# Sums of squares of queries and keys by a row product with 32 columns of ones on four column groups, then turned

## What is computed

```python
proj = hn @ w_in                                   # 256 x 4112
qkv = silu(causal_depthwise_conv(proj[..., :3 * 1024], conv_w))
def l2norm(x):
    return x * rsqrt(sum(x * x, axis=-1) + 1e-6)   # over the 128 features of a head
q = l2norm(heads(qkv[..., :1024])) * 128 ** -0.5
k = l2norm(heads(qkv[..., 1024:2048]))
v = heads(qkv[..., 2048:])
o = chunk_gated_delta_rule(q, k, v, g, beta)
```

## Time and profile before

| what | value |
|---|---|
| median of 3 runs | 1313.11 us (1312.80 to 1314.77) |
| the profiled execution's own time | 1314.13 us |
| its span, first to last instruction | 1312.4 us |
| mean granted clock of PE, 1 is full speed | 0.993 |
| PE busy | 1266.1 us, 96% of the span |
| DVE, ACT, POOL busy | 832.5, 666.7, 59.0 us |
| loads from HBM | 209.14 MB, 160 GB/s over the span |
| sums of squares on PE (L956) | 64 records (each product of float32 is two), 82.6 to 105.1 us |

### The profile page before, as it was taken

The page is one execution under the profiler, slowest core; times in us unless marked ns, Lnnn a source line. Parts: engine busy times, 40 slices in busy tenths (PEclk is TensorE's granted clock), DMA queues, the critical chain, the costliest instruction groups (busy, mean ns, idle before and its releaser), DMA issues.

```text
span 1312.4 us, 23625 instructions
## 1 busy us (share of the span) xinstructions
PE 1266.1 (96%) x9832; PEld 1184.1 (90%) x9832; DVE 832.5 (63%) x1133; ACT 666.7 (51%) x933; POOL 59.0 (4%) x102
## 2 busy tenths in 40 slices
PE   5999999999999999999999999999999988999997
PEld 5998898999998998899999999889999977999996
DVE  4875447655556555655556589987665566767664
ACT  4873656544445554444444554545454355654452
POOL 4000001000000001000000000010000010000000
PEclk9999999999999999999999999999999999999999
DMA  7650106665555644555554754443545642555550
GB/s 245 202 161 33 68 3 207 209 192 180 183 185 168 198 156 143 170 190 184 183 187 151 225 174 149 148 141 102 184 149 182 196 152 80 186 185 180 187 192 33
DMA packets 160471, 211.41 MB, mean 161 GB/s; under 512 B 5541, under 2 KB 143219, under 8 KB 160387
## 3 DMA queue, kind: packets, MB, share of 16 engines
q1 hardware_dynamic: 157299, 202.77, 48.2%
q0 software_dynamic: 2048, 7.37, 1.5%
q10 hardware_dynamic: 1040, 0.07, 0.1%
HBM read 209.14 MB, written 1.05 MB: 160 GB/s over the span
## 4 chain that ended last, share of the span: by engine, by line
PE 84%; DVE 8%; ACT 3%; issue 2%; DMA 1%; POOL 1%; DVEq 0%; SPq 0%; POOLq 0%; ACTq 0%
PE bank L306 25%; PE bank L309 25%; PE bank L310 25%; DVE wlo L300 2%; PE bank L1180 2%; PE bank L1200 1%; PE bank L1736 1%; ACT whi L292 1%; ACT common L544 1%; PE bank L1208 1%; DVE xlo L615 1%; DMA raw<-in_dn_w_in 1%; DVE common L2272 1%; PE bank L1818 1%; PE bank L2292 1%
## 5 line engine op out<-in xcount | busy, mean ns | idle before, releaser
L300 DVE TENSOR_TENSOR wlo<-raw,whi 128x2048 fp32r<-128x2048 f32 x191 | 437.0, 2290 | 240.2 <-ACT whi L292 239.8
L306 PE MATMUL bank<-xhi,whi 128*128 128x256 f32 x1824 | 524.7, 288 | 11.7 <-DVE xlo L615 11.3
L309 PE MATMUL bank<-xlo,whi 128*128 128x256 f32 x1824 | 517.9, 284 | 0.0
L310 PE MATMUL bank<-xhi,wlo 128*128 128x256 f32 x1824 | 517.8, 284 | 0.0
L292 ACT ACTIVATE whi<-raw 128x2048 fp32r<-128x2048 f32 x191 | 364.6, 1910 | 175.0 <-PE bank L306 121.6
L306 PEld LDWEIGHTS bank<-xhi,whi 128*128 128x128 f32 x1824 | 351.8, 193 | 17.5 <-issue 13.2
L309 PEld LDWEIGHTS bank<-xlo,whi 128*128 128x128 f32 x1824 | 351.8, 193 | 2.8 <-issue 1.2
L310 PEld LDWEIGHTS bank<-xhi,wlo 128*128 128x128 f32 x1824 | 351.7, 193 | 0.0
L306 PE MATMUL bank<-whi,hhi 128*128 128x512 f32 x392 | 154.0, 393 | 3.3 <-DVE hlo L2729 2.5
L309 PE MATMUL bank<-wlo,hhi 128*128 128x512 f32 x392 | 153.5, 392 | 0.0
L310 PE MATMUL bank<-whi,hlo 128*128 128x512 f32 x392 | 153.2, 391 | 0.0
(11 more groups left out here) (334 smaller groups left out, 1522.7 us busy)
## 6 DMA issues: line engine op xcount, KB each, us to landing
raw<-in_mlp_w_up SPq DMA_DIRECT2D x32, 1024.0 KB, 5.4
raw<-in_mlp_w_down SPq DMA_DIRECT2D x32, 1024.0 KB, 4.8
raw<-in_w_in SPq DMA_DIRECT2D x22, 1024.0 KB, 5.2
raw<-in_w_up SPq DMA_DIRECT2D x22, 1024.0 KB, 5.1
raw<-in_dn_w_in SPq DMA_DIRECT2D x16, 1024.0 KB, 5.7
raw<-in_w_gate SPq DMA_DIRECT2D x16, 1024.0 KB, 5.4
raw<-in_mb_w_in SPq DMA_DIRECT2D x12, 1024.0 KB, 5.1
raw<-in_w_down SPq DMA_DIRECT2D x11, 1024.0 KB, 4.8
```

What stands on the lines that cost most here:

```text
L300: nc.vector.tensor_tensor(wlo[:, s, :], raw[:, V % RAW, :], f32(whi[:, s, :]), ALU.subtract).then_inc(lo_ready, 1)
L306: ins = pe.matmul(o, shi, mhi, start=first, stop=False, skip_group_check=True)
L309: pe.matmul(o, shi, mlo, start=False, stop=False, skip_group_check=True)
L310: return pe.matmul(o, slo, mhi, start=False, stop=last, skip_group_check=True)
```

## The change

Per x (keys, queries) 16 products of one column become 8 products with `ones[:, 0:32]` as the stationary operand and a whole tile of squares (256 tokens) as the moving one. Four column groups `c` of 32 columns write four strips of 32 partitions of one bank, two heads `j` per strip, 256 columns each. ACT copies the bank to SBUF (`act_square_sums`, 128x512), PE turns four 128x128 blocks of it back into the same bank (`pe_turn_sums`), so that tokens lie on partitions again, and DVE picks every 32nd column in two instructions of 128x8.

The places: key sums after unit 9, turned after unit 10, and the query sums right behind; they are turned after unit 11. The copies stand in ACT's steps 10 and 11, behind the copy of the weight unit and before silu. Both sums and turns of the keys use bank 7 (`O[3]`), those of the queries bank 5 (`O[1]`, which was free until `pe_setup`). Nothing of the sums is left in `pe_setup` and `dve_setup`.

```diff
-            uss = {x: O[3].use() for x in (1, 0)}
+            uss = {1: O[3].use(), 0: O[1].use()}
+            ust = {1: O[3].use(), 0: O[1].use()}
+            sum_rows = [common[:, 512 * x:512 * x + 512] for x in range(2)]
...
-            def pe_square_sum(pe, x, n):
-
-                if n == 0 and uss[x].n:
-                    pe.wait_ge(uss[x].freed, uss[x].n)
-                t, hd = n // HN, n % HN
-                return pe.matmul(uss[x].ps[:, n:n + 1], sq[:, 8 * x + hd, t * P:(t + 1) * P], ones[:, 0:1],
-                                 start=(n == 0), stop=(n == 15), skip_group_check=True)
+            def pe_square_sums(pe, x):
+
+                use = uss[x]
+                if use.n:
+                    pe.wait_ge(use.freed, use.n)
+                pe.wait_ge(squares[4 * x + 3].sem, squares[4 * x + 3].value)
+                for j in range(2):
+                    for c in range(4):
+                        ins = pe.matmul(use.ps[32 * c:32 * c + 32, T * j:T * j + T], ones[:, 0:32],
+                                        sq[:, 8 * x + 2 * c + j, :], start=(j == 0), stop=(j == 1),
+                                        skip_group_check=True)
+                ins.then_inc(use.filled, 1)
+
+            def act_square_sums(act, x):
+                act.wait_ge(uss[x].filled, uss[x].n + 1)
+                nc.scalar.activation(sum_rows[x], uss[x].ps[:, :], ACT.Copy).then_inc(uss[x].freed, 1)
+
+            def pe_turn_sums(pe, x):
+                pe.wait_ge(uss[x].freed, uss[x].n + 1)
+                if ust[x].n:
+                    pe.wait_ge(ust[x].freed, ust[x].n)
+                for n in range(4):
+                    ins = pe.transpose(ust[x].ps[:, n * P:n * P + P], sum_rows[x][:, n * P:n * P + P], ident[:, :])
+                ins.then_inc(ust[x].filled, 1)
...
+                    elif u == 9:
+                        pe_square_sums(pe, 1)
+                    elif u == 10:
+                        pe_turn_sums(pe, 1)
+                        pe_square_sums(pe, 0)
+                    elif u == 11:
+                        pe_turn_sums(pe, 0)
...
                     split_hi(act, units[u])
+                    if u >= 10:
+                        act_square_sums(act, 11 - u)
...
-                elif u == 10:
-                    dve_square_means(dve, 1)
+                elif u >= 10:
+                    dve_square_means(dve, 11 - u)
...
-                dve.wait_ge(uss[x].filled, uss[x].n + 1)
-                nc.vector.tensor_scalar(msn[:, 16 * x:16 * x + 16], uss[x].ps[:, 0:16], EPS, None, ALU.add)\
-                    .then_inc(uss[x].freed, 1)
+                dve.wait_ge(ust[x].filled, ust[x].n + 1)
+                turned = ust[x].ps[:, :].rearrange("p (j t c r) -> p j t c r", j=2, t=NT, c=4)
+                heads = msn[:, 16 * x:16 * x + 16].rearrange("p (t c j) -> p j t c", t=NT, c=4)
+                for j in range(2):
+                    ins = nc.vector.tensor_scalar(heads[:, j], turned[:, j, :, :, 0], EPS, None, ALU.add)
+                ins.then_inc(ust[x].freed, 1)
...
                 pe_gram(pe, 1)
-                proj.pe_turn(pe)
                 pe_cross(pe, 1)
...
                 dve_first(dve, 0)
-                proj.dve_cum(dve)
                 dve_first(dve, 1)
```

More of the change, by code:

```diff
@@ L961, in pe_in @@
                 for u in range(12):
[L962 to L970, removed]
+                    gemm_features(pe, units[u], uses[u], xhi, xlo)
                     if u == 0:
@@ L1101, in pool_in @@
                     cs = slice(16 * x, 16 * x + 16)
-                    pool.wait_ge(uss[x].freed, uss[x].n + 1)
+                    pool.wait_ge(ust[x].freed, ust[x].n + 1)
                     nc.gpsimd.tensor_tensor(rsq[:, cs], msn[:, cs], mhalf[:, 0:16], ALU.pow).then_inc(roots[x].sem, 1)
             return Part(pe=pe_in, act=act_in, dve=dve_in, pool=pool_in, uc=(una, ugc, roots, gates_spread),
-                        pe_turn=pe_query_sums, act_copy=lambda act: finish_unit(act, 11),
-                        dve_cum=lambda dve: dve_square_means(dve, 0))
+                        act_copy=lambda act: finish_unit(act, 11))
         def z_block(j, bank):
```

## The result

| | before | after |
|---|---|---|
| median, runs side by side | 1313.94 us (1312.80 to 1315.51, 4 runs) | 1304.35 us (1303.89 to 1305.48, 4 runs) |
| ratio, 95% interval | | 0.9934 (0.9920 to 0.9947) |
| profiled execution: time, span | 1314.13, 1312.4 us | 1304.77, 1303.0 us |
| mean granted clock of PE | 0.993 | 0.998 |

What follows compares the result with a forecast made beforehand. PE was taken to bound the kernel, on the path for 84% of the span. Removing 8.60 us and adding 3.16 us gave -5.44 us, so 1313.1 - 5.4 = 1307.7 us, range 1306.0 to 1311.2 us.

Steps and rivals of the forecast that it cites:

- Key sums, 3.37 us, and query sums, 3.49 us, removed: On PE, one-column sums go: 3.37 us out of unit 10 and 3.49 us out of `pe_setup`.
- The slow stretch behind them, 1.74 us: PE work after the query sums, 105.18 to 109.03 us, returns to full clock: 1.74 us less.
- A set of sums, 1.04 us: Added on PE, twice: 16 passes on four column groups plus tile change there and back, 1.04 us a set.
- Turning, 0.54 us: Added on PE, twice: four transposes at 0.44 us, with 0.1 us for going in and out.
- Nobody is late: ACT's copies have 2.3 and 3.0 us of slack, DVE and bank 5 0.3 us; PE waits for none.
- my tightest place: Second gram product waiting for bank 5, free at 3.75 us and reached at 4.05 us: slack 0.3 us.
- First decays at 97.1 us, third 4.4 us earlier, first key product 5.4 us earlier: Expected in the changed profile: first decays hardly earlier than 97.30 us, third decays and first key product earlier as named.
- the sum of 5.44 us: Net on PE: 3.16 us added less 8.60 us removed, -5.44 us.
- PE's program after `pe_setup` is unchanged and shifts as a whole: Everything on PE behind `pe_setup` keeps its program and only moves with the net of -5.44 us.
- another slow stretch of the clock vanishing too: Rival: one more slow stretch of the clock goes, about 1306.0 us; chance 0.05.
- two groups of 64 columns side by side: In the old profile, 64-column tiles run 1.86 times as fast; four groups taken for the square sums, 0.86 us of passes.
- The slower case: Rival at the two sets of 16 passes: groups run serially with exposed weight loads, 3.2 us more, 1316.3 us; chance 0.03.

Runs made afterwards that it cites:

- the spread sums: Kernel before, with its 16 one-column query sums spread between the products of unit 11: 1311.51 us, ratio 0.9987.
- keys only: Kernel before, with only the key sums in the new form and the query sums left in the setup: 1311.04 us, ratio 0.9980.
- on the whole array: Changed kernel, with a 128-wide stationary operand and no column groups side by side: 1311.04 us, ratio 0.9977 to the kernel before.

## Why the forecast was too small

**Point by point, what was asked of the profile.**

1. *Key sums, 3.37 us, and query sums, 3.49 us, removed.* The query sums are right. The key sums were worth a little more, 9.21 + 5.84 - 2 x 5.75 = 3.55 us: the first product of unit 11 too came 0.08 us late behind them (91.46 to 91.66 us, where a product takes 0.12), and I had taken unit 11 as undisturbed.
2. *The slow stretch behind them, 1.74 us.* Right for these two traces, and settled by the spread sums: 1.68 us in the trace, -1.82 +- 0.98 us in the times. In one of the three traces with the old query sums it is 3.3 us, so in the mean over executions the term may be too small.
3. *A set of sums, 1.04 us.* It is 1.19 us. The passes side by side were right to the hundredth (4 x 0.216 = 0.86 us for 16 passes); the change to the narrow tile and back is 0.33 us, not 2 x 0.09. The row I took it from showed the way into tiles of 64 columns only, and I doubled it.
4. *Turning, 0.54 us.* It is 97.22 - 96.79 = 0.43 us, 0.11 us less, since the change of tile is within the 1.19 us. With 3., 0.1 us more than forecast in all, and with 1. the sum is where it was.
5. *Nobody is late.* PE has no idle time at either turning, and the second gram product doesn't wait for bank 5, my tightest place. DVE is through with the query sums at 100.4 us and PE is at that product at about 100.7 us: the slack of 0.3 us is as forecast.
6. *First decays at 97.1 us, third 4.4 us earlier, first key product 5.4 us earlier.* 97.22 us; 102.51 us, 4.3 us earlier against the same records of before; 104.81 instead of 110.10 us, 5.3 us earlier.

The distance to the start of the span hides a part of it: in the trace of the kernel after, unit 9 already starts 0.2 us later (76.63 instead of 76.42 us), ahead of anything that was changed. From there to the first key product it is 5.49 us less, and 5.50 us in the other pair of traces. So for `pe_setup` the sum of 5.44 us held to a tenth. DVE shows the same; its first instruction on the key product (L1513 of before) starts at 105.94 instead of 111.23 us.

**The step that failed** is one sentence of the prediction: "PE's program after `pe_setup` is unchanged and shifts as a whole." The program is unchanged, but it didn't shift as a whole. The same instructions, after against before:

| place, time of before | shift so far | what stands there |
|---|---|---|
| end of `pe_setup`, 111 us | -5.3 us | the change itself, 5.5 us, less the 0.2 us from ahead of it |
| inside the rounds of 64x64, 146 us | -6.0 us | a shorter wait of PE |
| end of the rounds, 165 us | -6.1 us | |
| 170 us | -7.5 us | half clock of before missing |
| 202 us | -8.8 us | half clock of before missing |
| 300 us | -8.4 us | some of it given back |
| 1093 us | -9.7 us | half clock of before missing |

So behind the change these two traces come apart by another 4.4 us; in the mean of all runs it is 1.9 us (7.4 - 5.5).

*The wait in the rounds* belongs to the change. PE's weight loads in the rounds; the bracket is idle time with nothing that the profile shows to wait for. Before, in the run shown first:

```profile
144.42 1.51 PEld L1200 LDWEIGHTS bank<-common 64*64 64x64 f32 x48 [1.20 <-issue]
...
150.15 0.20 PEld L1208 LDWEIGHTS bank<-ident,dn_x 64*64 64x64 f32 x4 [2.01 <-issue]
```

after (L1217 and L1225 are L1200 and L1208 of before):

```profile
139.09 0.83 PEld L1217 LDWEIGHTS bank<-common 64*64 64x64 f32 x25 [0.52 <-issue]
...
144.88 0.48 PEld L1225 LDWEIGHTS bank<-ident,common 64*64 64x64 f32 x13 [2.09 <-issue]
```

and the kernel with 20 spare products put in ahead:

```profile
142.31 1.97 PEld L1218 LDWEIGHTS bank<-common 64*64 64x64 f32 x64 [1.42 <-issue]
...
148.59 0.19 PEld L1226 LDWEIGHTS bank<-ident,common 64*64 64x64 f32 x4 [2.56 <-issue]
```

The gap stands at a fixed number of the instruction stream, not at a place of the program: in all 13 traces 1344 to 1346 weight loads stand ahead of it and 1468 to 1470 ahead of the second one. With 24 records fewer ahead of the rounds (32 + 8 for 64) it therefore sits 22 records later in them, with more ahead it sits earlier. With 25 records of L1217 left behind it in that block the gap is 0.52 us, 37 with 0.68 (keys only), 45 with 0.98 (10 spare products), 48 with 1.20 and 1.28, 64 with 1.42: the later it falls, the shorter. In another trace of the kernel after it is 0.33 us. So 24 records fewer ahead of the rounds are worth 0.7 to 0.9 us there. The second gap, 1.5 to 2.6 us, has no such order. From the first 64x64 record to 165 us of before, ahead of the slow stretch, it is 47.91 instead of 48.72 us, and 48.19 against 49.03 us in the second pair: 0.8 us.

I read this as the supply of PE's instructions, and the traces bear it out further than I had looked. The profile lists transfers of kind "instruction", on one queue (q8) 63 of 16 KB each. In all 13 traces both gaps end 1.1 to 1.5 us after one of these has landed: in the kernel before at 144.42 us after 142.96 us and at 150.15 after 148.80 us, in the kernel after at 139.09 after 137.67 and at 144.88 after 143.52 us. No experiment changed the supply alone, so this is supported and not shown.

*The half clock elsewhere* comes and goes in either kernel, as the second profile of the unchanged kernel shows, and so the three that the kernel after lacks in this pair of traces can't be put down to the change. Whether it makes them rarer is taken up in the account below. Most of these stretches stand behind idle time of PE: between 20 and 1280 us, those behind the query sums aside, the 13 traces hold 17 of 3.4 us at a clock of 0.50, and in the 3.4 us ahead of 12 of them PE was idle for 1.6 us or more. The one at 167 us isn't one of the 12: in the 3.42 us ahead of it PE was busy for 3.19 us, with small products. In the kernel before, PE alone (length, busy, records, clock):

```profile
190.00:194.00 4.00, 4.00 (x34) 1.00 0.00 0
194.00:197.60 3.60, 1.29 (x10) 1.00 0.33 82
1085.00:1088.50 3.50, 1.66 (x11) 1.00 0.58 202
```

and the same kernel again:

```profile
190.00:194.00 4.00, 2.43 (x21) 1.00 0.00 0
194.00:197.60 3.60, 2.86 (x23) 1.00 0.74 263
```

From 190.00 to 197.60 us PE is busy for 4.00 + 1.29 = 5.29 us in the one and 2.43 + 2.86 = 5.29 us in the other. After the same idle time the clock fell at 197.60 us in the one and not in the other. I gave "another slow stretch of the clock vanishing too" a chance of 0.05, at about 1306.0 us. It should have been several stretches of 1.4 to 1.6 us, in either kernel, by chance of the execution: the 87 runs of the kernel before go from 1309.5 to 1319.1 us. One profiled execution with a mean clock of 0.993 was taken as the kernel's; the prediction said that not all slow stretches were tied to the sums, but gave no spread for their coming and going.

**The account.** Of the 7.4 +- 0.9 us, 5.5 are the change as forecast, with 1.7 us of clock in it; 0.8 are the shorter wait in the rounds. Some 1.1 us are left, about as much as the interval. The clock can hold it. Each run has its mean granted clock on record: 0.9925 in 83 runs of the kernel before, 0.9954 in the 16 of the kernel after. Times the span, what is missing to 1 is 9.9 +- 0.5 us before and 6.0 +- 1.2 us after, so 3.9 +- 1.3 us fewer, where the one stretch of 3.4 us behind the query sums accounts for 1.7. Not all of it need be time, since PE is partly idle in some slow stretches (in the one from 16.5 to 23.3 us of the second profile of the kernel before it is busy for 5.64 of 6.80 us). Where the rest comes from stays open; the half clock at the query sums that lasted twice as long in one execution, for 1.6 us more, would be of this kind and direction, but how often it does so was not counted. The further 2.2 us of the first medians are chance: the first four runs of the changed kernel lie 1.7 us below the mean of all 16, and the four beside them 0.5 us above that of the kernel before.

*The groups and the loads.* The prediction had two groups of 64 columns side by side at 1.86 times and took four groups of 32 from them. Four groups gave 3.45 / 0.86 = 4.0 times for the passes, and 3.45 / 1.19 = 2.9 times with the change of tile. The slower case rested on a weight load in front of each pass. None is exposed: on the whole array 16 records with a load each took 3.45 us, 0.216 us each, as long as half a record of 512 columns (0.215 us), and each load (L962, 0.19 us) starts and ends while the record ahead of it runs.

## What to carry to other kernels

A reduction over partitions into one column per record cost PE 0.11 us a record (3.49 / 32), as much as a dense one of 128 columns (0.112 us), and 32 such records on end took the clock from 1.00 to 0.50. With 32 columns of ones on four column groups a set cost 1.19 us instead of 3.5 us, and 0.43 us for turning it; the groups, not the form, paid for it: without them a set cost 3.45 us. Before a gain of under 1% is costed, take two profiles of the unchanged kernel and line them up: what differs between them is no part of the sum but belongs in the range. And "the rest only shifts" is a claim to be tested where PE waits for nothing the profile shows, since here such waits stood at a number of the instruction stream and moved when records were taken out ahead of them.

## What the hardware showed beyond that

- Four column groups of 32 start within 20 ns of each other (82.556 to 82.576 us) and run at full speed side by side, 0.86 us for 16 records of 256 columns, where the whole array took 3.45 us; going to them and back costs 0.33 us, once for 16 or for 32 records.
- The same idle time of PE (2.31 us of 7.60) was followed by a stretch of 3.4 us at half the clock (0.51) in one execution and by none (1.00) in the next. One of 6.8 us at 0.50 stands near 16 us in five of the 13 traces, of either kernel.
- 32 one-column records on end brought the half clock (0.50) in all three traces that hold them, for 3.4 us in two and 6.8 us in one; spread between products the same records left it at 1.00.
- PE waits 0.3 to 2.6 us inside dense 64x64 work with no semaphore to wait for, at the same two numbers of the instruction stream in all 13 traces, and goes on 1.1 to 1.5 us after a transfer of instructions has landed. The first of the two waits went from 1.20 to 0.52 us with 24 records fewer ahead of it.
